# Reordering two engines' queues around the attention of a two-layer hybrid trunk

## Chip, cores and metric

One core of a Trainium2 chip runs the whole program. The metric is the device time of one execution in microseconds; lower is better. All arithmetic on the tensors here is in float32.

## What is computed

A chunk of 256 frames, with 16 learned meta tokens ahead of it, goes through two layers. Layer 0 is multi-head latent attention (MLA, 16 heads) followed by a mixture of experts, layer 1 is gated linear attention (GLA) followed by another mixture of experts. The change is in layer 0's attention:

```
z = h @ w_in;  c_q, c_kv, k_r = split(z)
q  = (rms_norm(c_q)  @ w_uq ).reshape(L, 16, 96)
kv = (rms_norm(c_kv) @ w_ukv).reshape(L, 16, 64 + 64);  k_nope, v = split(kv)
k  = concat(k_nope, broadcast(k_r))
q, k = rms_norm(q), rms_norm(k)          # sums of squares over the 96 of each head
q, k = rope on the last 32 of each
s = q @ k.T * scale, block-causal mask;  p = softmax(s);  o = p @ v;  out = o @ w_o
```

## The kernel before

Positions lie in three tiles: tile 0 and tile 1 of 128 frames each, and tile 2 with the 16 meta tokens, laid out four heads at a time (so its operations are smaller). Every engine has its own instruction stream in fixed program order, and they meet only through semaphores. Nothing is reordered at run time except what the semaphores allow.

**Projection and preparation.** TensorE works through the list `AJOBS`: q and k of tile 0, q and k of tile 1, q and kv of tile 2, v of tiles 0 and 1 (matmuls of L771, and of L713 for tile 2), and then the transposes of L785: `tq` of tile 0, `tk` of tile 0, `tq` of tiles 1 and 2, `tk` of tiles 1 and 2. The eight PSUM banks go round, so job j needs the copy that emptied job j - 8 (`a_empty`). ScalarE empties the q and tq jobs (`copies(i)`, L1145, and `turned(i)`, L1176 and L1178) and forms the squares of q (L1151) and of k (L1155). VectorE empties the k, kv and v jobs (`keys`, `meta_kept` at L1455 and L1458, `values_kept` at L1448) and the tk jobs (L1505), and sums the squares in `rotary(i)` (L1466 for q, L1474 and L1475 for k). ScalarE's `scales` turns the sums into reciprocal roots: Ln (L1162 for q, L1164 for k) and then Exp (L1167 for k, L1169 for q), which signals `k_rstd`. Each change from Ln to Exp or back costs a table load (ACT_TABLE_LOAD). With `k_rstd`, VectorE's `keys_scaled` (L1480) scales the 64 plain columns of k, and GpSimd's `keys_scaled` (L579) writes the 32 rotary ones, signalling `k_roped`. Only then can the tk transposes of tiles 1 and 2 run.

The dependences that set the order: ScalarE squares q of tile i only after `q_sums` says that VectorE has summed those of tile i - 1 (the squares share one buffer), and the k squares likewise wait for `k_sums`. `scales([1, 2], ...)` waits for the sums of tile 2. TensorE starts attention when all `AJOBS` are emptied, and SyncE starts the first experts' weights when all are transposed.

**Attention.** Heads go in pairs. With S(h) for the scores of head h (L796, L798), W(h) for the five transposes of its weights (L808 to L812), and V(p) for the values of pair p (L823 to L829), TensorE's order is: for each pair p, S(2p+2), W(2p), V(p-1), S(2p+3), W(2p+1). ScalarE has `exps(h)` (L1196, two exponentials with their accumulator reads), `meta_weights(h)` (L1205, copies the meta rows of the transposed weights) and `heads_out(p)` (L1209). VectorE has shift(h) (L1519 to L1521, the row maxima), scale(h) (L1525, L1528) and frame_weights(h) (L1535), in the order shift(2p+2), scale(2p+1), scale(2p+2), frame_weights(2p), shift(2p+3), frame_weights(2p+1).

V(p) waits for frame and meta weights of both of its heads. `exps(h)` waits for shift(h) and for W(h-2). `meta_weights(h)` waits for W(h) and, from head 2 on, for the values that last read its buffer.

After attention come the output projection with the router (L656), then the experts (L892, L872, L906, L914), for which SyncE streams 4 MB parts into a ring of slots (L486, L491), each when TensorE has read what lay there.

Of the kernel before, what the change touches and what calls it, by code (L numbers as in the profile page):

```python
# [23 lines left out]
ACT = mybir.ActivationFunctionType  # L24
# [95 lines left out]
def build(nc, a, out, ctx):  # L120
# [42 lines left out]
    eps_b, one_b = fix[:, 0:1], fix[:, 2:3]  # L163
# [13 lines left out]
    def take(*shape, kept=False):  # L177
        n = int(np.prod(shape))
        whole, end = (keep, SHARED) if kept else (arena, ARENA)
        assert top[kept] + n <= end, (top[kept], n)  # L180
        v = whole[:, top[kept]:top[kept] + n]
        top[kept] += n
        if len(shape) == 2:
            v = v.rearrange("p (a b) -> p a b", a=shape[0])
        if len(shape) == 3:
            v = v.rearrange("p (a b c) -> p a b c", a=shape[0], b=shape[1])
        return v
# [26 lines left out]
    junk = take(ROPE)  # L214
# [115 lines left out]
    def over(ap, n):  # L330

        return ap.unsqueeze(1).to_broadcast([ap.shape[0], n, ap.shape[1]])

    def flat(ap):
        return ap.rearrange("p a b -> p (a b)")
# [68 lines left out]
    def abank(j):  # L404
        return (j + 4) % 8
# [14 lines left out]
    def ajobs(kind, i):  # L420
        return [j for j, (k, t, _, _) in enumerate(AJOBS) if (k, t) == (kind, i)]
# [673 lines left out]
    def _(act):  # L1095
# [24 lines left out]
        def mla():  # L1120
# [18 lines left out]
            def copies(i):  # L1139

                H = HEADS if i < 2 else MH
                W = 512 if i < 2 else MH * QK
                for n, j in enumerate(ajobs("q", i)):
                    act.wait_ge(a_job, j + 1)
                    act.copy(flat(q_sb[i])[:, n * W:(n + 1) * W], ps[:, abank(j), 0:W]).then_inc(a_act, 1)  # L1145
                act.wait_ge(a_act, a_empty[j][1])
                if i == 0:
                    rotary_keys()
                else:
                    act.wait_ge(q_sums, i)  # L1150
                act.activation(sq[:, 0:H], q_sb[i], ACT.Square, scale=QK ** -0.5).then_inc(q_squared, 1)  # L1151
                act.wait_ge(*a_empty[ajobs("k" if i < 2 else "kv", i)[-1]])
                if i:
                    act.wait_ge(k_sums, i)
                act.activation(sqk[:, 0:H], k_sb[i][:, :, 0:NOPE], ACT.Square, scale=QK ** -0.5).then_inc(k_squared, 1)  # L1155

            def scales(tiles, queries):

                n = lambda i: slice(0, HEADS if i < 2 else MH)
                act.wait_ge(k_sums, tiles[-1] + 1)  # L1160
                for i in queries:
                    act.activation(qst[:, i, n(i)], qst[:, i, n(i)], ACT.Ln, scale=float(QK), bias=qbias[:, i:i + 1])  # L1162
                for i in tiles:
                    ins = act.activation(kst[:, i, n(i)], kst[:, i, n(i)], ACT.Ln)  # L1164
                link(ins)
                for i in tiles:
                    act.activation(krst[:, i, n(i)], kst[:, i, n(i)], ACT.Exp, scale=-0.5).then_inc(k_rstd, 1)  # L1167
                for i in queries:
                    act.activation(scl[:, i, n(i)], qst[:, i, n(i)], ACT.Exp, scale=-0.5)  # L1169

            def turned(i):
                for n, j in enumerate(ajobs("tq", i)):
                    act.wait_ge(a_job, j + 1)
                    src = ps[0:QK, abank(j), :].rearrange("p (h t) -> p h t", h=4)
                    if i < 2:
                        ins = act.copy(qT[0:QK, 4 * n:4 * n + 4, COL[i]:COL[i] + P], src)  # L1176
                    else:
                        ins = act.copy(qT[0:QK, :, 0:META].rearrange("p (j s) t -> p s j t", j=4),  # L1178
                                       src.rearrange("p s (j t) -> p s j t", j=4)[:, :, :, 0:META])
                    ins.then_inc(a_act, 1)  # L1180
# [2 lines left out]
            scales([0], [])  # L1183
            copies(1)
            copies(2)
            turned(0)
            scales([1, 2], [0, 1, 2])
            turned(1)
            turned(2)

# [10 lines left out]
            def meta_weights(hd):  # L1201
                act.wait_ge(p_turned, hd + 1)
                if hd >= 2:
                    act.wait_ge(pv_done, hd // 2)
                act.copy(pM[hd % 2][0:META, :], ps[0:META, 3 + 2 * (hd % 2), 0:SEQ]).then_inc(pt_act, 1)  # L1205
# [9 lines left out]
            exps(0)  # L1215
            exps(1)
            for hd in range(HEADS):
                if hd + 2 < HEADS:
                    exps(hd + 2)
                meta_weights(hd)  # L1220
                if hd and hd % 2 == 0:
                    heads_out(hd // 2 - 1)
            heads_out(HEADS // 2 - 1)
# [129 lines left out]
    def _(dve):  # L1353
# [44 lines left out]
        def mla():  # L1398
# [40 lines left out]
            def keys(i):  # L1439
                for n, j in enumerate(ajobs("k", i)):  # L1440
                    dve.wait_ge(a_job, j + 1)
                    dve.tensor_copy(k_sb[i][:, 8 * n:8 * n + 8, 0:NOPE], ps[:, abank(j), :].rearrange("p (h f) -> p h f", h=8))\
                        .then_inc(a_dve, 1)

            def values_kept(i):
                for n, j in enumerate(ajobs("v", i)):
                    dve.wait_ge(a_job, j + 1)
                    TS(vt[:, i, 8 * n:8 * n + 8, :], ps[:, abank(j), :].rearrange("p (h f) -> p h f", h=8),  # L1448
                       vsc[:, i:i + 1], None, ALU.mult).then_inc(a_dve, 1)

            def meta_kept():
                j, = ajobs("kv", 2)
                dve.wait_ge(a_job, j + 1)
                src = ps[:, abank(j), :].rearrange("p (h f) -> p h f", h=4)
                dve.tensor_copy(k_sb[2][:, :, 0:NOPE], src[:, :, 0:NOPE])  # L1455
                for q in range(4):
                    rows = slice(QUAD * q, QUAD * q + META)
                    ins = TS(vt[0:META, 2, MH * q:MH * (q + 1), :], src[rows, :, NOPE:], vsc[rows, 2:3], None, ALU.mult)  # L1458
                ins.then_inc(a_dve, 1)

            def rotary(i):

                Hn = HEADS if i < 2 else MH
                ra, rb_ = (rp[:, m].rearrange("p (h f) -> p h f", h=HEADS)[:, 0:Hn] for m in range(2))
                dve.wait_ge(q_squared, i + 1)
                dve.tensor_reduce(qst[:, i, 0:Hn], sq[:, 0:Hn], AX.X, ALU.add).then_inc(q_sums, 1)  # L1466
                if i == 2:
                    x = q_sb[i][:, :, NOPE:QK]
                    TT(ra, x, over(tcq[:, i, :], Hn), ALU.mult)
                    link(TT(rb_, x, over(tsq[:, i, :], Hn), ALU.mult))  # L1470
                    TT(q_sb[i][:, :, NOPE:NOPE + H], ra[:, :, 0:H], rb_[:, :, H:ROPE], ALU.subtract)
                    TT(q_sb[i][:, :, NOPE + H:QK], ra[:, :, H:ROPE], rb_[:, :, 0:H], ALU.add).then_inc(q_ready, 1)
                dve.wait_ge(k_squared, i + 1)
                link(dve.tensor_reduce(kst[:, i, 0:Hn], sqk[:, 0:Hn], AX.X, ALU.add))  # L1474
                TS(kst[:, i, 0:Hn], kst[:, i, 0:Hn], krx[:, i:i + 1], None, ALU.add).then_inc(k_sums, 1)  # L1475

            def keys_scaled(i):
                Hn = HEADS if i < 2 else MH
                dve.wait_ge(k_rstd, i + 1)
                TT(k_sb[i][:, :, 0:NOPE], k_sb[i][:, :, 0:NOPE], rep(krst[:, i, 0:Hn], NOPE), ALU.mult)\  # L1480
                    .then_inc(k_ready, 1)
# [3 lines left out]
            rotary(0)  # L1485
            dve.wait_ge(lat_pooled, 1)
            keys(1)
            meta_kept()
            rotary(1)
            rotary(2)  # L1490
            values_kept(0)
            values_kept(1)
            for i in range(3):
                if i == 1:
                    keys_scaled(1)
                    keys_scaled(2)
                for n, j in enumerate(ajobs("tk", i)):
                    dve.wait_ge(a_job, j + 1)
                    src = ps[0:QK, abank(j), :].rearrange("p (h t) -> p h t", h=4)
                    if i < 2:  # L1500
                        dst = kT[0:QK, 4 * n:4 * n + 4, COL[i]:COL[i] + P]
                    else:
                        dst = kT[0:QK, :, 0:META].rearrange("p (j s) t -> p s j t", j=4)
                        src = src.rearrange("p s (j t) -> p s j t", j=4)[:, :, :, 0:META]
                    TS(dst, src, gprod[0:QK, 0:1], None, ALU.mult).then_inc(a_dve, 1)  # L1505
# [348 lines left out]
```

## Time and profile before

| | |
|---|---|
| median of 3 runs | 745.5 us (744.25 to 747.52) |
| the profiled execution | 747.04 us, its span in the trace 744.9 us |
| busy share | PE 88%, PEld 51%, VectorE 34%, ScalarE 20%, GpSimd 5% |
| chain that ended last | PE 62%, DMA 29%, VectorE 3%, ScalarE 3%, issue 2% |
| projection and preparation for attention | about 11.6 to 83.8 us |
| attention loop | about 84 to 129 us |
| layer 0's experts | about 179 to 385 us |

The profile gives each engine's instructions with start and duration, and for each idle stretch the instruction that ended it. The chain that ended last is followed back from the last instruction; a stretch in it is one that set the end. PE is TensorE's matmul, PEld its weight load. Idle time of an engine that is not in the chain costs nothing. PEclk is the granted TensorE clock as a share of full speed.

### The profile page before, as it was taken

What the parts mean: (1) busy time and instruction counts of PE and PEld (TensorE: products, weight loads), DVE (VectorE), ACT (ScalarE), POOL (GpSimd) and SP (SyncE); (2) the same over time, 40 slices, a digit from 0 to 9 for tenths busy, and PEclk for the clock granted to TensorE, in tenths of its full rate; (3) what the DMA queues carried; (4) which work ended last, traced back from release to release, by engine and by line L of the source; (5) the groups of instructions that cost most, each with busy time, mean ns of one, the idle gap of its engine ahead of it and who ended that gap; (6) DMA issues with size and microseconds to landing.
All of it is one profiled execution on the core that took longest, in us unless ns stands there. A gap on an engine that the chain in (4) does not pass through costs nothing.

```text
span 744.9 us, 11318 instructions
## 1 busy us (share of the span) xinstructions
PE 654.9 (88%) x5001; PEld 381.8 (51%) x5001; DVE 251.2 (34%) x564; ACT 151.6 (20%) x309; POOL 38.0 (5%) x54
## 2 busy tenths in 40 slices
PE   6999788999999996977869999989999995866876
PEld 5654565457565643525338744464575552433422
DVE  2136786145323331321241641231353331311212
ACT  2143564433111000001020522032420000000000
POOL 1033100000000000000020410010000000000000
PEclk9999899999999998989889999999999998987989
DMA  9900551916999999999993135552869999999995
GB/s 327 419 13 1 226 226 29 422 31 273 426 438 434 424 427 436 427 427 432 428 429 167 59 167 212 240 226 110 337 274 433 427 435 431 421 435 435 421 426 217
DMA packets 12020, 234.05 MB, mean 314 GB/s; under 512 B 1520, under 2 KB 1840, under 8 KB 3136
## 3 DMA queue, kind: packets, MB, share of 16 engines
q1 hardware_dynamic: 11376, 232.68, 74.1%
q8 instruction: 43, 0.70, 0.4%
q10 hardware_dynamic: 592, 0.59, 0.2%
q14 instruction: 9, 0.07, 0.0%
HBM read 232.22 MB, written 1.05 MB: 313 GB/s over the span
## 4 chain that ended last, share of the span: by engine, by line
PE 62%; DMA 29%; DVE 3%; ACT 3%; issue 2%; POOL 0%; SPq 0%; DVEq 0%; ACTq 0%
DMA mem<-in_experts 28%; PE ps L892 10%; PE ps L1018 7%; PE ps L656 7%; PE ps L914 6%; PE ps L771 4%; PE ps L906 4%; PE ps L1009 4%; PE ps L872 3%; PE ps L723 3%; PE ps L713 1%; DMA mem<-in_mla_w_in 1%; PE ps L632 1%; PE ps L704 1%; PE ps L674 1%
## 5 line engine op out<-in xcount | busy, mean ns | idle before, releaser
L892 PE MATMUL ps<-mem,hT 128*32 128x256 f32 x1952 | 126.6, 409 | 32.3 <-DMA mem<-in_experts 31.4
L892 PEld LDWEIGHTS ps<-mem,hT 128*32 128x32 f32 x1952 | 67.9, 117 | 95.5 <-DMA mem<-in_experts 42.5
L1666 DVE TENSOR_TENSOR rows<-rows,ps 128x512 f32<-128x512 f32 (+1 forms) x80 | 54.8, 685 | 119.2 <-PE ps L914 119.2
L914 PE MATMUL ps<-hT,mem 128*128 128x512 f32 x160 | 76.4, 609 | 3.4 <-DVE hT L1660 1.8
L906 PE MATMUL ps<-mem 128*32 128x512 f32 x496 | 63.9, 649 | 11.8 <-DMA mem<-in_experts 7.3
L872 PEld LDWEIGHTS ps<-mem,rows 128*128 128x128 f32 x560 | 63.6, 192 | 5.8 <-issue 5.8
L872 PE MATMUL ps<-mem,rows 128*128 128x128 f32 x560 | 66.2, 278 | 0.0
L1250 ACT ACTIVATE mem<-ps 128x256 f32<-128x256 f32 x16 | 9.9, 621 | 244.4 <-PE ps L892 244.4
L656 PE MATMUL ps<-mem,hT 128*128 128x512 f32 x128 | 57.1, 598 | 2.9 <-ACT hT L1330 2.9
L1018 PE MATMUL ps<-mem,hT 128*128 128x512 f32 x128 | 55.6, 594 | 0.0
L914 PEld LDWEIGHTS ps<-hT,mem 128*128 128x128 f32 x160 | 24.0, 170 | 50.3 <-issue 50.3
L1018 PEld LDWEIGHTS ps<-mem,hT 128*128 128x128 f32 x128 | 24.2, 190 | 29.9 <-issue 29.8
L656 PEld LDWEIGHTS ps<-mem,hT 128*128 128x128 f32 x128 | 23.6, 190 | 30.5 <-issue 29.3
L906 PEld LDWEIGHTS ps<-mem 128*32 128x32 f32 x496 | 16.0, 115 | 45.1 <-issue 41.0
L1651 DVE TENSOR_TENSOR hT<-ps,gn 128x512 f32<-128x512 f32 x32 | 21.9, 689 | 37.4 <-PE ps L872 37.4
L1660 DVE COPY hT<-ps 128x512 f32<-128x512 f32 x16 | 11.1, 691 | 66.6 <-PE ps L906 66.6
L1656 DVE TENSOR_TENSOR mem<-mem,ps 128x256 f32<-128x256 f32 x16 | 9.8, 610 | 65.7 <-ACT mem L1250 65.7
L771 PE MATMUL ps<-mem 128*128 128x512 f32 x68 | 31.7, 624 | 0.0
L1009 PE MATMUL ps<-hT,mem 128*128 128x256 f32 (+1 forms) x128 | 29.8, 393 | 0.0
L1009 PEld LDWEIGHTS ps<-hT,mem 128*128 128x128 f32 x128 | 24.6, 194 | 5.1 <-issue 0.9
L632 PE MATMUL ps<-cst,rows 128*128 128x128 f32 (+1 forms) x88 | 14.1, 318 | 10.6 <-DMA rows<-in_x 6.1
L771 PEld LDWEIGHTS ps<-mem 128*128 128x128 f32 x68 | 13.3, 198 | 17.3 <-issue 17.2
(277 smaller groups left out, 668.3 us busy)
## 6 DMA issues: line engine op xcount, KB each, us to landing
mem<-in_experts SPq DMA_DIRECT2D x36, 4096.0 KB, 34.9
mem<-in_experts SPq DMA_DIRECT2D x20, 2048.0 KB, 17.5
mem<-in_gla_parts SPq DMA_DIRECT2D x4, 4096.0 KB, 23.4
rows<-in_experts SPq DMA_DIRECT2D x4, 2048.0 KB, 36.4
mem<-in_mla_o SPq DMA_DIRECT2D x1, 4096.0 KB, 33.0
mem<-in_mla_w_in SPq DMA_DIRECT2D x2, 1344.0 KB, 12.1
mem<-in_mla_uq SPq DMA_DIRECT2D x1, 2304.0 KB, 20.0
mem<-in_mla_ukv SPq DMA_DIRECT2D x1, 2048.0 KB, 23.9
```

The source lines that it names most:

```text
L632: mm = pe.transpose(dst, src[0:R, k, :], ident[0:R, 0:R])
L656: mm = pe.matmul(ps[:, OUT[l][2 * i + b], :], hT[:, k, META + i * P:META + (i + 1) * P], w[:, k, b * 512:(b + 1) * 512], start=k == 0, sto ...
L723: mm = pe.matmul(ps[:, (5 + m) % 8, 0:POS], wz[:, k, m * P:(m + 1) * P], hT[:, k, :], start=k == 0, stop=k == KD - 1)
L771: mm = pe.matmul(ps[:, b, :], cT[:, k, COL[i]:COL[i] + P], w, start=m == 0, stop=k == ks[-1])
L872: mm = pe.matmul(ps[:, k // 4, (k % 4) * P:(k % 4 + 1) * P], xn[:, i, k, :], Sg[:, i, :], start=i == 0, stop=i == nt - 1)
L892: mm = pe.matmul(ps[32 * j:32 * j + 32, 2, m * FE:(m + 1) * FE], xe[:, k, 32 * j:32 * j + 32], w[:, j, c * FE:(c + 1) * FE], start=k == 0 ...
L906: mm = pe.matmul(ps[32 * j:32 * j + 32, 5 + b, :], hidT[:, k, 32 * j:32 * j + 32], w[:, j, k, :], start=k == 0, stop=k == 1)
L914: pe.matmul(ps[0:WID[i], banks[nt * b + i], :], back[:, COL[i]:COL[i] + WID[i]], ysb[:, b * 512:(b + 1) * 512], start=True, stop=True).the ...
L1009: mm = pe.matmul(b[:, 0:POS - c0], wqk[:, k, o:o + GDK], hT[:, k, c0:POS], start=k == 0, stop=k == KD - 1)
L1018: mm = pe.matmul(b[0:WID[i], :], hT[:, k, COL[i]:COL[i] + WID[i]], w[:, k, hb * 512:(hb + 1) * 512], start=k == 0, stop=k == KD - 1)
L1651: TT(xe[:, 4 * b:4 * b + 4, :], ps[:, b, :].rearrange("p (k q) -> p k q", k=4), rep(gn[:, norm_n, 4 * b:4 * b + 4], P), ALU.mult).then_inc ...
L1666: TT(hh, hh, ps[0:WID[i], banks[nt * b + i], :], ALU.add).then_inc(K.add, 1)
```

## The change

On ScalarE, `scales([1, 2], [0, 1, 2])` moves ahead of `turned(0)`, the copies of the transposed queries of tile 0. Ahead of it stands one new Ln on a single element, whose result is not used and whose table load runs where it stands. In attention, for odd heads `meta_weights(hd)` is issued ahead of `exps(hd + 2)` instead of behind it.

On VectorE, `rotary(1)` moves ahead of `meta_kept()`, and the two `keys_scaled` calls move from between the tk copies of tile 0 and tile 1 to ahead of those of tile 0. What is computed stays the same.

```diff
@@ ScalarE, preparation @@
             copies(1)
             copies(2)
+            act.activation(junk[0:1, 0:1], one_b[0:1], ACT.Ln)
+            scales([1, 2], [0, 1, 2])
             turned(0)
-            scales([1, 2], [0, 1, 2])
             turned(1)
             turned(2)
@@ ScalarE, attention @@
             for hd in range(HEADS):
+                if hd % 2:
+                    meta_weights(hd)
                 if hd + 2 < HEADS:
                     exps(hd + 2)
-                meta_weights(hd)
+                if hd % 2 == 0:
+                    meta_weights(hd)
                 if hd and hd % 2 == 0:
                     heads_out(hd // 2 - 1)
@@ VectorE, preparation @@
             keys(1)
+            rotary(1)
             meta_kept()
-            rotary(1)
             rotary(2)
             values_kept(0)
             values_kept(1)
+            keys_scaled(1)
+            keys_scaled(2)
             for i in range(3):
-                if i == 1:
-                    keys_scaled(1)
-                    keys_scaled(2)
                 for n, j in enumerate(ajobs("tk", i)):
```

## Rows read from the trace of the kernel before

**Rows 1.** Chain that ended last, tile rotation: start us, us, engine, line.
```profile
71.85 2.04 ACT mem L1176 x4
...
73.90 1.28 ACT L1162
...
75.20 0.69 ACT mem L1162 x3
...
77.70 2.11 POOL mem L579
```

**Rows 2.** TensorE in order of time: start, us, line, shapes, [idle before <-releaser].
```profile
79.90 2.36 PE L785 MATMUL ps<-cst,mem 128*96 128x128 f32 x20 [2.57 <-POOL mem L579]
```

**Rows 3.** VectorE in order of time, same columns.
```profile
64.38 0.42 DVE L1455 COPY mem<-ps 128x256 f32<-128x256 f32 x1 [3.13 <-PE ps L713]
...
66.69 1.75 DVE L1466 TENSOR_REDUCE mem<-mem 128x16 f32<-128x1536 f32 x1
...
69.75 0.55 DVE L1466 TENSOR_REDUCE mem<-mem 128x4 f32<-128x384 f32 x1
...
71.72 2.73 DVE L1448 TENSOR_SCALAR mem<-ps,mem 128x512 f32<-128x512 f32 x4
...
77.65 2.42 DVE L1480 TENSOR_TENSOR mem<-mem 128x1024 f32<-128x1024 f32 x2 [0.58 <-ACT mem L1167]
80.55 3.11 DVE L1505 TENSOR_SCALAR mem<-ps,mem 96x512 f32<-96x512 f32 x5 [0.47 <-PE ps L785]
```

**Rows 4.** ScalarE in order of time, same stretch.
```profile
61.28 1.06 ACT L1155 ACTIVATE mem<-mem 128x1024 f32<-128x1024 f32 x1 [2.06 <-DVE mem L1442]
...
68.54 0.52 ACT L1151 ACTIVATE mem<-mem 128x384 f32<-128x384 f32 x1 [5.41 <-DVE mem L1466]
69.94 0.42 ACT L1155 ACTIVATE mem<-mem 128x256 f32<-128x256 f32 x1 [0.87 <-DVE mem L1475]
...
77.62 0.40 ACT L1169 ACTIVATE mem<-mem 128x16 f32<-128x16 f32 x3
```

**Rows 5.** All engines in order of time, one pair of heads.
```profile
102.70 0.27 PE L808 MATMUL ps<-cst,mem 128*128 128x128 f32 x1
...
102.90 0.31 DVE L1519 TENSOR_REDUCE mem<-ps 128x1 f32<-128x144 f32 x1 [0.22 <-PE ps L798]
...
103.67 0.56 DVE L1535 COPY mem<-ps 128x384 f32<-128x384 f32 x1
...
103.79 0.47 ACT L1196 ACTIVATE mem<-ps,mem 128x144 f32<-128x144 f32 x1 [1.09 <-DVE mem L1521]
...
104.15 0.31 DVE L1519 TENSOR_REDUCE mem<-ps 128x1 f32<-128x144 f32 x1
...
104.81 0.34 ACT L1205 COPY mem<-ps 16x256 f32<-16x256 f32 x1
...
105.06 0.46 ACT L1196 ACTIVATE mem<-ps,mem 128x144 f32<-128x144 f32 x1
...
105.25 0.29 PE L823 MATMUL ps<-mem 128*64 128x16 f32 x4 [0.58 <-issue]
...
106.20 0.17 DVE L1525 RECIPROCAL mem<-mem 128x2 f32<-128x2 f32 x1 [0.49 <-ACT mem L1196]
...
106.88 0.55 DVE L1535 COPY mem<-ps 128x384 f32<-128x384 f32 x1
...
109.96 0.29 PE L823 MATMUL ps<-mem 128*64 128x16 f32 x4 [0.58 <-issue]
```

**Rows 6.** Busy time by stretch: A:B length, engines, PEclk, DMA share, GB/s.
```profile
80.00:90.00 10.00, 7.15 (x70) 5.30 (x70) 7.01 (x23) 2.67 (x10) 0.90 (x3) 0.81 0.68 270
...
102.00:128.00 26.00, 21.72 (x187) 16.67 (x187) 19.42 (x67) 15.09 (x54) 0.00 (x0) 1.00 0.06 23
```

**Rows 7.** Waits of SyncE's DMA queue: total us, times, longest.
```profile
SPq L491 <- ACT hT L1209: 45.6, 1, 45.6
```

**Rows 8.** Chain that ended last, layer 0's experts.
```profile
254.33 38.36 DMA mem<-in_experts
```

## The prediction

> **What bounds the kernel now.** I read the chain that ended last first, then each engine in order of time at the two places that the change touches, then the busy time by stretch and the waits of the DMA queue, to see whether time won there reaches the end.
>
> In the preparation the chain runs over TensorE's matmuls until the first transposes. Then it leaves TensorE: ScalarE's four query copies from 71.85, a table load at 73.90, the logarithms at 75.20, and GpSimd's rotary key columns from 77.70 for 2.11 us [rows 1]. TensorE meanwhile stands idle for 2.57 us and starts the last 20 transposes at 79.90 [rows 2]. VectorE ends its last copy at 80.55 + 3.11 = 83.66 [rows 3], and attention starts behind that. So the reciprocal roots of the keys of tiles 1 and 2 come too late. They wait for ScalarE's copies, but also for the sums: VectorE waits 3.13 us idle for tile 2's kv job at 64.38, runs the meta copies, and only at 66.69 sums tile 1's squares. ScalarE sits idle for 5.41 us because of that sum [rows 3, 4].
>
> In the attention loop one pair of heads takes 109.96 - 105.25 = 4.71 us. The reader is to see what stands just ahead of the values at 105.25: ScalarE's meta copy at 104.81, which had the exponentials of 103.79 in front of it, and those had waited for VectorE's shift. What the copy reads, the transposes of 102.70, was long there [rows 5].
>
> **Does the time reach the end?** While attention runs, the DMA engines are 6% busy, and the queue waits 45.6 us for the last head output before it issues more experts [rows 6, 7]. Layer 0's experts become bound by transfers only at 254.33 [rows 8], and those transfers were triggered by TensorE's own progress after attention. Nothing later starts at a time of its own. I pass the whole gain through.
>
> **Part 1, the sums.** VectorE's keys of tile 1 are emptied when ScalarE starts their squares at 61.28; these take 1.06, to 62.34 [rows 4]. `rotary(1)` takes 69.75 - 66.69 = 3.06 us [rows 3]. In the idle stretch it runs from 61.25 to about 64.35, and the meta copies start as before at 64.4, since they wait for TensorE. They take 66.69 - 64.38 = 2.31, to 66.7. The cost is nothing, because 3.13 us of idle time covers it; without that cover it would be 3.06. ScalarE's square of tile 2's q (0.52) now follows the sum at about 63.0, and that of its k (0.42) follows the meta copies, 66.8 to 67.2 [rows 4]. `rotary(2)` takes 71.72 - 69.75 = 1.97 [rows 3]: 66.7 to 68.7, three us earlier than before.
>
> **Part 2, the scales.** The new one-element Ln loads its table at 67.2, to 68.5; a load took 75.20 - 73.90 = 1.30 [rows 1]. The Ln itself is about 0.2, by the small exponentials of rows 4 (0.40 for three, overlapping). Before, the whole block ran from 73.90 to 77.62 + 0.40 = 78.02, 4.12 us [rows 1, 4]. Without its first load it is 2.82: 68.75 to 71.55, with `k_rstd` out at about 71.2 (in the block before, the keys' users started at 77.65 to 77.70, 0.35 from its end [rows 1, 3]). The first query copy can't start before 71.85 anyway [rows 1]. So the scales cost the copies nothing, with 0.3 us to spare; each us beyond that delays the copies by one.
>
> At this place a rule speaks against the change. The row shows no gap behind a table load: 1.30 us from load to logarithm [rows 1]. The Trainium skill, "ScalarE: Activation LUTs", section "What ACT_TABLE_LOAD costs", adds a drain of about 1.38 us to the load of 1.283. By it the copies would start at 74.3, and the sum would be about 1.5 us less; that is rival (e).
>
> **Part 3, the key scaling.** VectorE's four value copies took 71.72 to 74.36 for all four [rows 3]. Now they start at 68.7, and the last waits for TensorE's last v job (71.4): they end at about 72.1. Then `keys_scaled` of both tiles: 2.42 us in the trace, of which part is waiting, since GpSimd's two L579 ran at the same time and the first took 2.11 [rows 1, 3]. GpSimd starts at 71.2 now, mostly ahead of VectorE. I take 2.3, to 74.4, which is when the tk copies of tile 0 started before (71.72 + 2.73 = 74.45). Ends: done sooner it buys nothing, since the last five copies wait for transposes from 77.33 on; with the full 2.42 it is 0.1 late, and 0.9 would still be covered. GpSimd's `k_roped` comes at 73 to 74, before TensorE wants it at 77.33.
>
> **The sum of the preparation.** TensorE's idle 2.57 goes: the last 20 transposes start at 79.90 - 2.57 = 77.33 [rows 2]. VectorE has then just ended the tile 0 copies (74.4 + 2.7 = 77.1) and takes the last five 0.65 behind the transposes as before, 78.0 to 81.1. What is late next is VectorE itself, with 0.9 us of slack. Gain 83.66 - 81.1 = 2.6. The ends are 1.1, with ScalarE held as in rival (e), and 2.7.
>
> **Part 4, the loop.** With the odd head's meta copy ahead, it runs when the transposes of 102.70 are done, at about 103.5, where ScalarE was idle for 1.09 us up to 103.79 [rows 5]. It lasts 0.34, so the exponentials start at most 0.05 late, and as the values (and the odd transposes behind them) come up to 0.9 sooner against VectorE's work, there are some 0.7 us to spare. The values then wait for VectorE's frame weights (103.67 + 0.56, plus 0.1 for the semaphore, an estimate) instead of 105.25: start of frame weights to values 0.66 instead of 1.58, gained 0.9 once. What is late next is a ring of VectorE and ScalarE that TensorE isn't in: frame weights to shift 0.48 (103.67 to 104.15), shift to exponentials 0.89 (102.90 to 103.79), exponentials to scale 1.14 (105.06 to 106.20), scale to frame weights 0.68 (106.20 to 106.88), frame weights to the odd shift 0.48, shift to frame weights 0.77 (102.90 to 103.67): 4.44 us [rows 5]. That is 0.27 less than 4.71, five times between pair 1 and the last: 1.35. The last two heads give back about 0.1. In the first pair the exponentials do wait for the meta copy (about 0.5), which falls into VectorE's slack there. Sum 0.9 + 1.35 - 0.1 = 2.15. The ends: TensorE's own work, 21.72 of 26 us [rows 6], is 3.9 of 4.71 per pair and isn't reached; the most would be 0.9 + 5 x 0.8 = 4.9. The least is 0, were the meta copies to hold up the exponentials by as much as they free.
>
> **Total.** 2.6 + 2.15 = 4.75. The profiled run took 747.04 (span 744.9) and would be 742.3. It lies 1.5 over the median of the three, so against the median: 745.5 - 4.75 = 740.7.
>
> **The rivals.** (a) The gain is taken back by the transfers, 745.5: if the experts' streams were limited from their start. Against it: 6% DMA share in attention and the wait of 45.6 us [rows 6, 7]. 0.10.
>
> (b) One part does nothing: the scales come late or the ring is longer than I add up. About 742.9 with the preparation alone, 743.3 with the loop alone. For it: 0.3 us of slack in part 2 and 0.7 in part 4. 0.12 together.
>
> (c) The clock helps. The granted clock was 0.81 in the mean of 80 to 90 us, part at the lower of the two levels, 1.2 GHz, right behind the idle stretch that goes [rows 2, 6]. TensorE was busy 7.15 us there. A mean of 0.81 is 0.38 of 10 us at half speed, 3.8 us of which 1.9 would go at 2.4 GHz; about two thirds of it lies on the path, 1.3 us: 739.4. 0.14.
>
> (d) Slower, by the clock. The waits fall elsewhere and the lower level holds through attention. TensorE's 21.72 us of 26 become 43.4 and bound the loop, so each us at 1.2 GHz costs 1 - 26/43.4 = 0.40. From 12 us more of it than before the gain is gone, from 21 the kernel is 0.5% slower; all of that stretch at 1.2 GHz gives 740.7 + 17.4 = 758. For it: the drop to 0.81 at the start of attention. Against: 1.00 from 102 to 128 with more idle time than will be left [rows 6]. 0.04.
>
> (e) ScalarE stands still behind each table load, as long again as the load (1.30). Both loads ahead of the copies are passed, so `k_rstd` comes at 73.8 instead of 71.2. VectorE then has 2.6 less, 0.9 of it slack and some 0.2 of it idle time ahead of the last value copy; 1.5 stays: 742.2. Against it: the logarithm of 75.20 right behind the load of 73.90 [rows 1]. 0.03.
>
> **How the numbers follow.** The forecast has 0.57, (a) 0.10, (b) 0.12, (c) 0.14, (d) 0.04, (e) 0.03. The range of 8 in 10 reaches from 738.4, below (c), to 744.2, above (b) and (e); (a) and (d) are left out. A measurement tells about 0.5% (3.7 us) from no change, so faster means below 741.8: 0.85 of the forecast, all of (c), a little of (b), together 0.65. Slower is (d), 0.03. The rest, 0.32, is within 0.5%, and most of it would still be a real gain of 2 to 3.5 us.
>
> **What would show it.** No idle of TensorE ahead of the last 20 transposes; the scales' exponentials done before the first L1176; `keys_scaled` ahead of the first L1505; attention's first scores 2.6 earlier; a pair period of 4.4 with values released by L1535 and no longer by L1205; the last head output 4.75 earlier, and the same lead at the first expert matmul and at the end. It is wrong if a gap appears behind a table load, if L1196 starts over 0.3 behind its shift in steady pairs, or if the lead shrinks between 129 us and the end.

## The result

| | kernel before | changed kernel |
|---|---|---|
| median beside each other | 744.99 us (6 executions) | 739.27 us (6 executions) |
| ratio, 95% interval | | 0.9892 (0.9858 to 0.9927) |
| profiled execution, its span | 747.04 us, 744.9 us | 741.55 us, 739.5 us |
| all executions of this study | median 747.3 us (73) | median 739.8 us (18) |

The kernel is faster, by 5.7 us by the first medians and by 7.5 us over all executions. The forecast was 4.75 us. Its sign and both mechanisms hold, but the measured ratio lies beyond the low end of its range (738.4 of 745.5 is 0.9905, which lies inside the interval). The ratios leave out three executions that took over 1.5% more than the fastest of their kernel (747.06, 746.38 and 747.08 us), the medians count them.

Single executions of either kernel spread over some 12 us, so I read the sizes from spans inside the traces, and the medians only as a check on them. The page of the changed kernel, its span and its clock line:

```profile
span 739.5 us, 11319 instructions
...
PEclk9989899999999998988999999999999998997989
```

The chain that ended last, in the preparation (start us, us, what):

```profile
72.80 7.86 PE ps L785 x72
80.66 1.51 issue
82.17 0.45 PE ps L836 x29
```

The 72 transposes are now one piece of 7.86 us without a hole. The piece that stood in between before [rows 1, 2] is gone. From the first transpose to the first scores it is 82.17 - 72.64 = 9.53 us, where it was 83.77 - 71.21 = 12.56 (both first transposes by TensorE's timeline): 3.03 us less. The profiled execution had reached its first transpose 1.43 us later than the one of before, ahead of anything that the change touches: it had 6.8 us at 1.2 GHz in the projection where the one of before had 3.4.

VectorE in order of time, same stretch:

```profile
62.59 1.74 DVE L1470 TENSOR_REDUCE mem<-mem 128x16 f32<-128x1536 f32 x1
...
65.81 0.42 DVE L1459 COPY mem<-ps 128x256 f32<-128x256 f32 x1
...
68.12 0.55 DVE L1470 TENSOR_REDUCE mem<-mem 128x4 f32<-128x384 f32 x1
...
73.51 1.78 DVE L1484 TENSOR_TENSOR mem<-mem 128x1024 f32<-128x1024 f32 x2
75.21 2.71 DVE L1508 TENSOR_SCALAR mem<-ps,mem 96x512 f32<-96x512 f32 x4
78.95 3.11 DVE L1508 TENSOR_SCALAR mem<-ps,mem 96x512 f32<-96x512 f32 x5 [1.03 <-PE ps L785]
```

Against [rows 3]: tile 1's sums (62.59) now fill the time ahead of the meta copies (65.81), which start right behind them. Key scaling (73.51) is over before the key copies of tile 0 (75.21), and VectorE then waits 1.03 us for the last transposes. ScalarE in order of time:

```profile
64.60 0.53 ACT L1151 ACTIVATE mem<-mem 128x384 f32<-128x384 f32 x1
68.13 0.42 ACT L1155 ACTIVATE mem<-mem 128x256 f32<-128x256 f32 x1 [3.00 <-DVE mem L1462]
68.56 1.28 ACT L1186 ACT_TABLE_LOAD   x1
69.86 0.20 ACT L1186 ACTIVATE mem<-fix 1x1 f32<-1x1 f32 x1
...
71.01 1.28 ACT L1167 ACT_TABLE_LOAD   x1
72.31 0.31 ACT L1167 ACTIVATE mem<-mem 128x16 f32<-128x16 f32 x2
...
73.28 2.04 ACT L1176 COPY mem<-ps 96x512 f32<-96x512 f32 x4 [0.35 <-PE ps L785]
```

Against [rows 4]: the square of tile 2's q follows at once (64.60), where it had 5.41 us of idle time ahead of it. The exponentials (72.31) are over before the first query copy (73.28), which has waited 0.35 us for TensorE. That is the slack of 0.3 that the prediction gave it.

One pair of heads in order of time, all engines (L1538 is the old L1535, L1522 the old L1519, L1528 the old L1525, L1197 the old L1196, L1206 the old L1205):

```profile
101.00 0.28 PE L808 MATMUL ps<-cst,mem 128*128 128x128 f32 x1
...
101.39 0.56 DVE L1538 COPY mem<-ps 128x384 f32<-128x384 f32 x1
...
101.51 0.47 ACT L1197 ACTIVATE mem<-ps,mem 128x144 f32<-128x144 f32 x1 [0.65 <-DVE mem L1524]
101.87 0.30 DVE L1522 TENSOR_REDUCE mem<-ps 128x1 f32<-128x144 f32 x1
...
102.01 0.29 PE L823 MATMUL ps<-mem 128*64 128x16 f32 x4 [0.29 <-DVE mem L1538]
...
102.75 0.47 ACT L1197 ACTIVATE mem<-ps,mem 128x144 f32<-128x144 f32 x1
...
103.90 0.17 DVE L1528 RECIPROCAL mem<-mem 128x2 f32<-128x2 f32 x1 [0.46 <-ACT mem L1197]
...
104.58 0.55 DVE L1538 COPY mem<-ps 128x384 f32<-128x384 f32 x1
...
104.91 0.36 ACT L1206 COPY mem<-ps 16x256 f32<-16x256 f32 x1 [0.52 <-PE ps L812]
...
105.05 0.30 DVE L1522 TENSOR_REDUCE mem<-ps 128x1 f32<-128x144 f32 x1
...
105.81 0.56 DVE L1538 COPY mem<-ps 128x384 f32<-128x384 f32 x1
...
106.43 0.29 PE L823 MATMUL ps<-mem 128*64 128x16 f32 x4 [0.30 <-DVE mem L1538]
```

Against [rows 5]: the odd head's meta copy (104.91) follows its transposes at once, the exponentials come behind it, and the values (102.01, 106.43) are released by VectorE's frame weights (101.39, 105.81), 0.62 later. The period is 106.43 - 102.01 = 4.42 us.

At the end of attention the first projection matmul (L713) starts at 124.56 us, before at 128.84: 4.28 earlier, and 5.71 with the 1.43 that were lost ahead of the change. The lead then holds. In the chain that ended last, the place where layer 0's experts become bound by transfers:

```profile
250.05 38.19 DMA mem<-in_experts
```

This answers [rows 8]: 254.33 - 250.05 = 4.28 again. At the end it is 744.9 - 739.5 = 5.4, a little more than was carried in; behind L713 the changed kernel's trace spent 51.4 us at 1.2 GHz, the one of before 58.1.

### The profile page after: what moved, and what is told of

Same layout as the page of the kernel before. It is cut to its first block, busy times and chain, and to the rows that moved or that the text cites. A ratio compares the mean times of both kernels' runs of the same rounds, so it can differ in the third digit from the quotient of the medians.

```text
span 739.5 us, 11319 instructions
## 1 busy us (share of the span) xinstructions
PE 653.7 (88%) x5001; PEld 382.3 (52%) x5001; DVE 250.2 (34%) x564; ACT 152.7 (21%) x310; POOL 37.7 (5%) x54
## 4 chain that ended last, share of the span: by engine, by line
PE 60%; DMA 30%; DVE 5%; ACT 2%; issue 2%; SPq 0%; DVEq 0%; ACTq 0%
DMA mem<-in_experts 28%; PE ps L892 10%; PE ps L1018 7%; PE ps L656 7%; PE ps L914 6%; PE ps L771 4%; PE ps L906 4%; PE ps L1009 4%; PE ps L872 3%; PE ps L723 3%; PE ps L713 1%; DMA mem<-in_mla_w_in 1%; PE ps L632 1%; ACT mem L1197 1%; PE ps L785 1%
## 5 line engine op out<-in xcount | busy, mean ns | idle before, releaser
L892 PE MATMUL ps<-mem,hT 128*32 128x256 f32 x1952 | 126.6, 410 | 33.6 <-DMA mem<-in_experts 32.8
L892 PEld LDWEIGHTS ps<-mem,hT 128*32 128x32 f32 x1952 | 68.7, 118 | 96.0 <-DMA mem<-in_experts 44.1
L914 PE MATMUL ps<-hT,mem 128*128 128x512 f32 x160 | 76.4, 609 | 3.4 <-DVE hT L1663 1.8
L906 PE MATMUL ps<-mem 128*32 128x512 f32 x496 | 62.0, 633 | 11.1 <-DMA mem<-in_experts 6.8
L914 PEld LDWEIGHTS ps<-hT,mem 128*128 128x128 f32 x160 | 24.0, 170 | 49.5 <-issue 49.5
L771 PEld LDWEIGHTS ps<-mem 128*128 128x128 f32 x68 | 13.7, 206 | 17.8 <-issue 17.8
```

The lines of the kernel that those rows point to most:

```text
L771: mm = pe.matmul(ps[:, b, :], cT[:, k, COL[i]:COL[i] + P], w, start=m == 0, stop=k == ks[-1])
L892: mm = pe.matmul(ps[32 * j:32 * j + 32, 2, m * FE:(m + 1) * FE], xe[:, k, 32 * j:32 * j + 32], w[:, j, c * FE:(c + 1) * FE], start=k == 0 ...
L906: mm = pe.matmul(ps[32 * j:32 * j + 32, 5 + b, :], hidT[:, k, 32 * j:32 * j + 32], w[:, j, k, :], start=k == 0, stop=k == 1)
L914: pe.matmul(ps[0:WID[i], banks[nt * b + i], :], back[:, COL[i]:COL[i] + WID[i]], ysb[:, b * 512:(b + 1) * 512], start=True, stop=True).the ...
```

## Experiments

The tables give spans from each kernel's own trace: from the first transpose (L785) to the first scores (L836), the steady pair period, and from the first scores to the projection (L713), with the time in it at the lower clock level.

| kernel | L785 to L836 | period | L836 to L713 | of it at 1.2 GHz | median us (executions) |
|---|---|---|---|---|---|
| before | 12.56 | 4.71 | 45.07 | 6.8 | 744.99 (6) |
| changed | 9.53 | 4.42 | 42.39 | 6.8 | 739.27 (6) |
| e1_whole | 9.53 | 4.42 | 41.35 | 0 | 738.28 (6) |
| e2_prep | 9.53 | 4.71 | 45.63 | 3.4 | 744.06 (7) |
| e3_loop | 12.56 | 4.42 | 41.35 | 0 | 742.21 (12) |
| e4_ring | 9.53 | 4.06 | 39.80 | 6.8 | 738.79 (6) |
| e5_sums_only | 12.55 | 4.71 | 45.10 | 6.8 | 743.88 (1) |
| e6_late_sums | 11.50 | 4.42 | 42.38 | 6.8 | 740.46 (1) |
| e7_no_first_ln | 9.53 | 4.42 | 41.35 | 0 | 740.28 (1) |
| e8_filled | 9.49 | 4.42 | 41.33 | 0 | 742.27 (9) |
| e9_null | 12.58 | 4.71 | 46.06 | 11 | 747.63 (12) |
| e10_whole_again | 9.53 | 4.42 | 42.39 | 6.8 | 740.45 (6) |
| e11_ring_again | 9.53 | 4.05 | 39.77 | 6.8 | 742.62 (12) |

The kernel before beside them had 748.36 us (18 executions) for e1 to e4, 747.22 (14) for e5 to e8 and 746.47 (23) for e9 to e11.

### The whole, and each part alone

**e1_whole** is the changed kernel as it stands.

> The changed kernel once more, against the kernel before on the same chip. Theory A (all of the gain is made ahead of the output projection): the trace gives 5.7 us, 3.0 in the preparation (83.77 to 82.17, with 1.43 us that the profiled run of after had lost already before the first transpose) and 2.7 in the loop, and the medians differ by 5.7; ratio 0.9923, in 0.990 to 0.995. Theory B (the ratio of 0.9892 is the true size, some 2.3 us come from elsewhere, such as the transfers): ratio 0.989 or less, and the lead grows by over 2 us between the first L713 behind attention and the end. In the trace both expect a lead of 5.7 at that L713 against equal clocks ahead of the change.

Ratio 0.9858 (0.9818 to 0.9899), below theory A's range and within theory B's (0.989 or less): 748.36 to 738.28. The spans are those of the first trace, the loop shorter by 1.04 us since no stretch at 1.2 GHz fell into it. From L713 to the end it is 617.4 us, against 616.1 before and 614.9 in the first trace of the change. So the lead doesn't grow behind attention, and theory B's place is wrong, but its size isn't refuted by this run.

**e2_prep** leaves the loop's part out:

```diff
-                if hd % 2:
-                    meta_weights(hd)
                 if hd + 2 < HEADS:
                     exps(hd + 2)
-                if hd % 2 == 0:
-                    meta_weights(hd)
+                meta_weights(hd)
```

> Only the preparation's part: sums, scales and key scaling as changed, the odd heads' meta weights behind the exponentials as before. Theory A: the scores of head 0 follow the last v matmul by 9.4 us instead of 12.4, the pair period is 4.71 as before, total 3.0 us faster, ratio 0.9960. A rival (the two parts share one cause, the clock at the start of attention): under 1.5 us, over 0.998, and the whole gain comes only with both parts.

The preparation shows its 9.53 us and the loop its old 4.71. Ratio 0.992 (0.9884 to 0.9957), where 0.9960 was expected. Its 3.4 us at 1.2 GHz fell on the first pair of heads, whose period was 6.34 us there where the kernel before has 4.75 and e5 4.76: 1.6 us lost.

**e3_loop** is that part alone, on the kernel before:

```diff
             for hd in range(HEADS):
+                if hd % 2:
+                    meta_weights(hd)
                 if hd + 2 < HEADS:
                     exps(hd + 2)
-                meta_weights(hd)
+                if hd % 2 == 0:
+                    meta_weights(hd)
```

> Only the loop's part: the odd heads' meta weights ahead of the exponentials, the preparation as before. Theory A: pair period 4.42, values released by VectorE's frame weights, last head output 2.7 us earlier against the first scores, total 2.7 us faster, ratio 0.9964; together with the preparation alone it adds up to the whole within 1 us. The forecast's own term was 2.15 (ratio 0.9971); it is too small if the first pair's exponentials don't wait for the meta copy.

12.56 us of preparation as before, period 4.42. Ratio 0.9931 (0.9903 to 0.9958), where 0.9964 was expected. So both ratios show more than the traces; together they take off 1.49%, and the whole took off 1.42% beside the same executions of before. The parts are independent: each leaves the other's span as it was. With the same 6.8 us at 1.2 GHz in the same place the loop's worth is 45.07 - 42.39 = 2.68 us (42.39 again in e10, 42.38 in e6, 45.10 without it in e5), and the preparation's is 3.03 in all of its pairs. Together 5.71.

### What the preparation needs

**e5_sums_only** moves only VectorE's sums.

```diff
             keys(1)
+            rotary(1)
             meta_kept()
-            rotary(1)
```

> The kernel before with only VectorE's sums of tile 1 moved ahead of the meta copies. Theory: the scales still stand behind ScalarE's query copies, which TensorE releases, so k_rstd and all behind it keep their times: from the first transpose to the first scores 12.3 to 12.6 us, as before. Rival (the sums were what made the scales late): 11 us or less.

12.55 us: nothing. ScalarE in order of time shows why. Its first load runs at 72.11, behind the four query copies, though the sums were ready, and the exponentials come at 75.61, 6.2 us behind the first transpose (69.41):

```profile
72.11 1.28 ACT L1162 ACT_TABLE_LOAD   x1
...
74.32 1.28 ACT L1167 ACT_TABLE_LOAD   x1
75.61 0.31 ACT L1167 ACTIVATE mem<-mem 128x16 f32<-128x16 f32 x2
```

**e6_late_sums** is the changed kernel with the opposite edit, the sums back behind the meta copies.

> The changed kernel with VectorE's sums of tile 1 back behind the meta copies; the scales stay ahead of the query copies. Theory: the sums of tile 2 are ready 0.5 us after the first transpose instead of 2.5 ahead of it, the scales end some 3.5 us after it, the query copies start about 2.9 late, and VectorE's key copies follow: from the first transpose to the first scores about 11.0 us, against 9.5 of the changed kernel and 12.6 of before. Rival (ScalarE's order does it alone): 9.5.

11.50 us, so without the sums the rest (ScalarE's order and the earlier key scaling together) is worth 1.06, and the sums are worth 1.97 on top. Neither the scales nor the key scaling was run alone. I had expected 11.0. VectorE in order of time has all nine key copies in one piece of 5.74 us, so it had become the bound:

```profile
75.35 5.74 DVE L1508 TENSOR_SCALAR mem<-ps,mem 96x512 f32<-96x512 f32 x9
```

It is 2.7 + 3.1 us of copies as in the changed kernel, but they begin at 75.35, 5.66 behind the first transpose, where they begin 2.57 behind it in the changed kernel; 1.03 of that is slack there.

**e7_no_first_ln** leaves out the new one-element Ln:

```diff
             copies(2)
-            act.activation(junk[0:1, 0:1], one_b[0:1], ACT.Ln)
             scales([1, 2], [0, 1, 2])
```

> The changed kernel without the one-element Ln. Two answers: if the table load runs where it stands, ahead of the wait for the sums, it hides as before, the scales end within 0.2 us of where they did and 9.5 us stay. If it runs behind the wait, the scales end 1.3 us later, the query copies start about 0.9 us late, and the time from first transpose to first scores stays 9.5 to 9.7, since VectorE's keys have 1.0 us of slack. I expect the first: in tile 0 the load ran ahead of a wait of 0.8 us.

9.53 us. ScalarE in order of time:

```profile
65.69 1.28 ACT L1162 ACT_TABLE_LOAD   x1
67.23 0.69 ACT L1162 ACTIVATE mem<-mem 128x16 f32<-128x16 f32 x3 [0.26 <-DVE mem L1478]
...
70.41 2.04 ACT L1176 COPY mem<-ps 96x512 f32<-96x512 f32 x4 [0.35 <-PE ps L785]
```

The load at 65.69 runs before the logarithms, which then wait 0.26 us for VectorE's sums. It starts 4.08 us ahead of the first transpose, as the load of the changed kernel does (68.56 and 72.64). The load stands ahead of the wait already, so this line of the change does nothing.

### What bounds the loop now

**e4_ring** moves one call of VectorE in the changed kernel:

```diff
                 scale(2 * hp + 1)
+                frame_weights(2 * hp)
                 if more:
                     scale(2 * hp + 2)
-                frame_weights(2 * hp)
```

> The changed kernel with one edit more: VectorE issues the even head's frame weights ahead of the next even head's scaling, in the time in which it waits for the exponentials. If the ring of VectorE and ScalarE (0.48 + 0.89 + 1.14 + 0.68 + 0.48 + 0.77 = 4.44) bounds the loop after the change, the period falls to the next bound, values to frame weights 1.51, 0.48, scaling 0.68, shift 0.77, frame weights to values 0.62, together about 4.07, and the kernel is 5 to 6 x 0.35 = about 2 us faster than the changed one (ratio to before 0.9897 if that one has 0.9923). If TensorE or the transfers bound it, the period stays at 4.42 and the time doesn't move.

All engines in order of time:

```profile
101.94 0.56 DVE L1538 COPY mem<-ps 128x384 f32<-128x384 f32 x1
...
102.41 0.30 DVE L1522 TENSOR_REDUCE mem<-ps 128x1 f32<-128x144 f32 x1
...
102.55 0.29 PE L823 MATMUL ps<-mem 128*64 128x16 f32 x4
...
104.08 0.56 DVE L1538 COPY mem<-ps 128x384 f32<-128x384 f32 x1
...
104.56 0.15 DVE L1528 RECIPROCAL mem<-mem 128x2 f32<-128x2 f32 x1
...
105.99 0.56 DVE L1538 COPY mem<-ps 128x384 f32<-128x384 f32 x1
...
106.61 0.29 PE L823 MATMUL ps<-mem 128*64 128x16 f32 x4
```

Period 106.61 - 102.55 = 4.06 us, as worked out (4.07). The even frame weights (104.08) now fill the time in which VectorE waited for the exponentials. So the ring of VectorE and ScalarE was the bound of the changed loop. The loop is 42.39 - 39.80 = 2.6 us shorter. The time isn't: 738.79 beside 738.28.

**e11_ring_again** repeats it.

> The kernel with VectorE's even frame weights ahead of the scaling, a second time, beside the changed kernel on the same chip. The traces give it 2.6 us over the changed one (period 4.06 instead of 4.42, first scores to the output projection 39.8 instead of 42.4 with the same low stretch); the first medians showed none of that (738.79 and 738.28). Theory A: 2 to 3 us under the changed kernel's median, ratio to before 0.988 or less. Rival (the time won in the loop is given back by the transfers or the clock later): same time as the changed kernel.

Median 742.62 beside 740.45 of the changed kernel; ratio to before 0.9917 (0.9883 to 0.9952). Over all executions of the two kernels the means are 740.65 (18 executions, standard error 0.9) and 739.8 (18, 0.6). The executions that the ratios count have means of 739.9 and 739.4. The 2.6 us are in both traces and not in the times. Part of it can be seen: in both traces a stretch of 6.8 us at 1.2 GHz fell on layer 0's last experts (365 to 373 us), where two of the changed kernel's three traces had none, and L713 to the end took 617.8 and 617.4 us against 614.9, 614.9 and 617.4. But it is not this kernel's alone: 7 of the 13 traces of this study have such a stretch there, e1 and e7 too, and with equal stretches most of the ring's gain is there at the end. From the first transpose to the end e4 took 667.2 us and e11 666.7, with 6.8 us at 1.2 GHz in the loop and 6.8 in the experts; e1 took 668.3 with none in the loop, by estimate 669.3 with the loop's 1.04. Two traces can't tell whether the stretches come more often with this kernel, so why the times don't show the 2.6 us is open. By the times the changed kernel is no worse, and I keep it.

### Is some of the gain clock?

**e9_null** is the kernel before against itself.

> The kernel before itself, measured as if it were a change: what the method makes of no change. If the spread of 735 to 753 us is chance in every execution (stretches at 1.2 GHz that fall elsewhere each time), the ratio is within 0.997 and 1.003 and its interval is some 0.003 to either side. If it comes out beyond 0.996, ratios of this size say little on their own, and the 0.9892 and 0.9858 of the change are no evidence for more than the 5.7 us of the traces. In its profile the time from first transpose to first scores is 12.56 and the pair period 4.71.

Ratio 1.0007 (0.9977 to 1.0038), so the method shows no change where there is none, and the ratios of the change aren't its error. Its trace shows something that the first one of before didn't. TensorE by stretch (A:B, length, busy, PEclk, DMA share, GB/s), at the preparation's end:

```profile
76.00:80.00 4.00, 1.89 (x15) 0.92 0.01 4
80.00:84.00 4.00, 3.38 (x43) 0.50 0.46 131
```

The same stretches of e1_whole, the changed order:

```profile
76.00:80.00 4.00, 2.49 (x49) 1.00 0.43 131
80.00:84.00 4.00, 2.39 (x13) 1.00 1.04 451
```

In e9_null the kernel before went to half speed at 79.4 us and stayed there until 93, 13.7 us in all. TensorE's row shows what it did:

```profile
78.11 3.28 PE L785 MATMUL ps<-cst,mem 128*96 128x128 f32 x20 [2.58 <-POOL mem L579]
```

It had stood idle for 2.58 us up to 78.11, and the clock fell 1.3 us into the last transposes. Up to the first scores this cost nothing (12.58 us), and the whole way from first scores to projection took 1.0 us longer than in its first trace. The changed kernel has no such idle stretch. Its traces had 6.8, 0, 6.8 and (e7) 0 us from the first scores to the projection, those with the old preparation 6.8, 0 (e3), 6.8 (e5) and 11: too few to tell.

**e10_whole_again** was to tell the two sizes apart.

> The changed kernel a third time, beside the null measurement. Theory A (5.7 us, all ahead of the output projection): ratio 0.992 +- 0.003. Theory B (8 us or more, some of it through a higher mean granted clock): ratio 0.989 or less, with a mean clock over its runs at least 0.003 above that of the kernel before, as 0.957 against 0.953 so far.

Ratio 0.9914 (0.9881 to 0.9946), mean granted clock over its executions 0.9573. It lies between the two theories. Each execution also lists its mean clock, so I fitted all 134 that have one with a level for each run (one for all executions of the kernel before) and one slope for all. The slope is 484 us for a whole unit of mean clock (standard error 36), 0.33 us for each us at 1.2 GHz. At one mean clock of 0.955 the kernel before stands at 746.8 (0.2), the changed one at 740.5, 740.9 and 741.5 (0.7 each), mean 741.0: 5.8 us apart, close to the 5.71 of the traces. The mean clock was 0.9537 before and 0.9573 after, and that difference times 484 is 1.8 us. So by this fit about 1.8 of the 7.5 us over all executions go with the clock, and 5.7 are order. The fit is not a proof: at equal clock it puts the ring kernel (e4, e11) 0.6 us (standard error 0.6) below the changed one, where the traces have 2.6, and e8 (below) 2.9 us (0.7) above it, with the same spans in the trace up to the projection.

**e8_filled** puts dummy transposes into TensorE's waits at the start of attention, to keep the clock up there:

```diff
             pe.wait_ge(a_act, a_counts["act"])
+            for _ in range(12):
+                pe.transpose(ps[:, 6, 0:P], ident, ident)
             pe.wait_ge(a_dve, a_counts["dve"])
...
+            for _ in range(6):
+                pe.transpose(ps[:, 6, 0:P], ident, ident)
             pe.wait_ge(mq_p, 1)
...
             mm.then_inc(mq_t, 1)
+            for _ in range(8):
+                pe.transpose(ps[:, 5, 0:P], ident, ident)
             pe.wait_ge(mq_c, 1)
```

> The changed kernel with 12, 6 and 8 transposes of the identity more, whose result nothing reads, where TensorE waits ahead of and in the first heads of attention. Theory C (part of the measured gain is clock: fewer stretches at 1.2 GHz around the start of attention): the granted clock is 1.00 from the first transposes to the first head outputs in the profile, first scores to end of the loop takes 41.35 us as in the whole kernel's undisturbed trace and not 42.4, and the median falls 0.5 to 1.5 us below the changed kernel's. Rival (the clock plays no part): same time as the changed kernel within its interval or, if the added transposes stand in the way, up to 0.5 slower, and low stretches there as often as before.

The granted clock was 1.00 from 76 to 120 us and the span 41.33, both as theory C had it. The median was not: 742.27, ratio to before 0.9944 (0.9911 to 0.9977), and mean clock 0.9564, no higher than the changed kernel's. The median lies 1.8 to 4.0 us above the three of the changed kernel (739.27, 738.28, 740.45), not below them, and more than the 0.5 that the rival allowed; its trace shows no place that costs so much. So the lower level at the start of attention costs the 1.04 us that e1 and e10 show, filling it in made the kernel no faster, and where the changed kernel's higher mean clock comes from is open.

## Why the prediction was right or wrong

- **What bounds it, and that the time reaches the end:** right. The lead at L713 (4.28) is the lead at the first transfer-bound part (4.28). Rival (a) fell.
- **Part 1, the sums:** right. `rotary(1)` from 62.59 to 65.7 hides ahead of the meta copies at 65.81; e5 and e6 show that it is worth 1.97 us, and only with the other parts.
- **Part 2, the scales:** right, slack 0.35 where 0.3 was given. The new Ln was costed with a load that it is meant to bring forward; e7 shows that the load stood early without it. There is no gap behind a load: 68.56 + 1.28 to the Ln at 69.86, and 71.01 + 1.28 to 72.31. Rival (e) fell. The Trainium skill, "ScalarE: Activation LUTs", section "What ACT_TABLE_LOAD costs", gives the same 1.28 for the load but adds a drain of 1.38; here the measurement decides, and none is seen.
- **Part 3, the key scaling:** VectorE took 1.7 us for it (73.51 to 75.21), where I took 2.3. GpSimd's first L579 had begun 0.91 us ahead of it (72.60) and took 1.07 us, where before the two engines began within 0.05 us and it took 2.10. The scaling ends in time for the slack of 1.03 to cover it, though no run moved it alone.
- **The sum of the preparation:** mis-sized, 2.6 against 3.03. The step that failed is "the last 20 transposes start at 79.90 - 2.57 = 77.33". I removed only the hole that the row of TensorE shows. TensorE in order of time, before and then changed:

```profile
71.21 3.93 PE L785 MATMUL ps<-cst,rows 128*96 128x128 f32 x32
74.98 2.35 PE L785 MATMUL ps<-cst,mem 128*96 128x128 f32 x20
```

```profile
72.64 3.66 PE L785 MATMUL ps<-cst,rows 128*96 128x128 f32 x32
76.13 4.53 PE L785 MATMUL ps<-cst,mem 128*96 128x128 f32 x40
```

The first 32 transposes took 74.98 - 71.21 = 3.77 us, start to start, and now 76.13 - 72.64 = 3.49. The difference of 0.28 is mostly one wait: the last four of the 32 need the bank that VectorE's last value copy empties, at 74.45 before [rows 3], and those copies now come earlier, as in e5, which has 3.49 too. The other 0.18 or so is no wait: where no hole follows, transposes overlap (the first row before ends at 71.21 + 3.93 = 75.14, and the next starts at 74.98), so one unbroken piece is shorter than two added up. That is 0.46 us beside the hole of 2.57. My walk through VectorE had the earlier copies in it (values done at 72.1 instead of 74.4) without asking who waits for them.
- **Part 4, the loop:** mechanism and ring right (4.44 forecast, 4.42 measured, and e4 moved the next bound to where it was worked out), size 2.15 against 2.68. The term that was mis-sized is "five times between pair 1 and the last: 1.35". From the first pair's values to the seventh's there are six periods, 28.29 us before and 26.49 now: 1.80. The other terms nearly hold: the first pair's values come 11.01 us behind the first scores instead of 12.03 (1.02 against 0.9), and the last pair gives back 0.13 (against 0.1). Behind the count of five stood the step "in the first pair the exponentials do wait for the meta copy", which failed. All engines in order of time, first pair of the changed kernel:

```profile
91.46 0.36 ACT L1206 COPY mem<-ps 16x256 f32<-16x256 f32 x1 [0.60 <-PE ps L812]
...
91.80 0.30 DVE L1522 TENSOR_REDUCE mem<-ps 128x1 f32<-128x144 f32 x1
...
92.69 0.47 ACT L1197 ACTIVATE mem<-ps,mem 128x144 f32<-128x144 f32 x1 [0.86 <-DVE mem L1524]
...
93.17 0.29 PE L823 MATMUL ps<-mem 128*64 128x16 f32 x4 [0.44 <-DVE mem L1538]
```

The meta copy at 91.46 is done 0.9 us before the exponentials of 92.69, which wait for VectorE's shift of 91.80 and not for it. So the first pair gives nothing back: its values are already ahead by the whole step, and the period behind it is as short as the others.

- **Rival (c), the clock:** I set it aside as an alternative with a chance of 0.14, for the first heads only. It came on top of the forecast, not instead of it. If the fit is right, it is the largest missing term over all executions, 1.8 us, against 0.4 and 0.5 for the other two; what raises the mean clock stays open. What I had as evidence was one profiled execution, in which the kernel before spent 6.8 us there at 1.2 GHz; e9_null had 11. Taking the forecast and (c) as exclusive cases also set the range's low end too high: 740.7 less 1.8 and less 0.9 for the two terms is 738.0, outside it.
- **Rivals (b) and (d):** neither came. The preparation and the loop each bring their time alone (e2, e3), and no trace had the lower level through attention. Of (d)'s price of 0.40 us for each us at 1.2 GHz in the loop, e2 bears out the order of size: 1.6 us for 3.4, or 0.47.

## What to carry to other kernels

When a wait is removed, look at who else was served late by the engine that is now earlier; the hole in the chain is only the largest of them. When a loop is bound by two engines that hand work to each other, add up the ring of their starts: it gave the new period to 0.02 us twice, and told which call to move next, though the times of that kernel then did not fall. Where executions spread by 1%, take sizes from spans between two marks in traces that have the same stretches at the lower clock in the same places, and treat a change in those stretches as a term of its own that adds to them.

## What the runs showed of the hardware

The granted clock fell while TensorE was busy the whole time. In the changed kernel's trace it dropped at 43.1 us, among 72 small matmuls (L742 and L745, 1 to 32 columns each) of which 23 had started, and stayed down in the wide ones behind them:

```profile
44.00:48.00 4.00, 4.00 (x36) 0.50 0.00 0
```

There it stayed for 6.8 us. e4, e10 and e11 had the same drop, with 24 of the 72 started. e8 had 3.4 us from there, before 3.4 us from 1.1 us behind the small matmuls on, and e1, e2, e3, e5, e6, e7 and e9 none. So the same program pays for it in some executions and not in others.

What a us at 1.2 GHz costs depends on where it falls, and three places can be read off:

- In the projection, where TensorE doesn't wait, about half. From the first small matmul to the first transpose it is 28.77 us in the seven traces without a drop, 30.33 and 30.47 in the two with 3.4 us of it, and 31.98 to 32.02 in the four with 6.8.
- In the first heads of attention, ahead of the first values, 1.04 us for 6.8, since TensorE waits there for the other engines.
- In layer 0's experts, 2 to 3 us for one stretch. From their first L892 to their last L914 it is 203.4 to 204.2 us in the seven traces with 6.8 us at 1.2 GHz that start between 362 and 370 us, and 201.3 to 202.1 in the other six.

Over the whole kernel the fit has 0.33 us for each us. From the projection behind attention to those experts all traces took 50.7 us, and behind them they agree within 1.2 us. So most of what the traces differ by, beside the change itself, lies ahead of it (the first transpose comes at 67.65 to 74.34 us) and in layer 0's experts.
